# Sums over features in the norms of a three-layer fp32 block: additions on GpSimd, then two matmuls, in place of eight matmuls

## The reference

```python
def layer_norm(x, g, b):                       # end of layers 1 and 2
    mu = jnp.mean(xf, axis=-1, keepdims=True)
    var = jnp.mean(jnp.square(xf - mu), axis=-1, keepdims=True)
    return (xf - mu) * lax.rsqrt(var + LN_EPS) * g + b

x_new = layer_norm(DEEPNORM_ALPHA * x + gate * y, ln_g, ln_b)     # y: the layer's output projection

def rmsnorm(x, g):                             # layer 3: four of these
    return xf * lax.rsqrt(jnp.mean(xf * xf, axis=-1, keepdims=True) + RMS_EPS) * g
```

## Time and profile before

| | |
|---|---|
| median of 3 runs | 3994.05 us (3992.76 to 3996.78) |
| profiled execution: first to last instruction | 3989.9 us |
| what lies around the span (median less span) | 4.15 us |
| TensorE matmuls busy | 3558.6 us (89%) |
| DVE, ACT, POOL busy | 1573.4 us (39%), 1315.7 us (33%), 70.2 us (2%) |
| mean granted TensorE clock | 0.932 of 2.4 GHz |

### The profile page before, as it was taken

One profiled execution on the slowest core, in us unless ns is written; L12 is line 12 of the kernel. 1 busy time (PEld: TensorE's weight loads), 2 busy tenths in 40 slices (PEclk: granted clock), 3 DMA queues, 4 the chain that ended last, 5 costly groups with the idle time before them and its releaser, 6 DMA issues.

```text
span 3989.9 us, 45425 instructions
## 1 busy us (share of the span) xinstructions
PE 3558.6 (89%) x18676; PEld 2754.5 (69%) x18676; DVE 1573.4 (39%) x3007; ACT 1315.7 (33%) x2213; POOL 70.2 (2%) x113
## 2 busy tenths in 40 slices
PE   9988888988979889988968889789888899999997
PEld 8866667767847667666737677666656678777885
DVE  3333343344354334444334455533333433323322
ACT  3122233333262223433353323322322433323322
POOL 1000000000000000000000000000000000000000
PEclk9988899898989889999989999899977999999998
DMA  5111101103331000102320000000001222223222
GB/s 199 64 39 40 54 22 44 44 22 113 103 109 43 27 32 22 32 22 74 108 81 28 17 17 17 27 22 27 27 16 48 79 91 95 76 88 111 95 90 69
DMA packets 61709, 232.57 MB, mean 58 GB/s; under 512 B 7162, under 2 KB 7288, under 8 KB 60736
## 3 DMA queue, kind: packets, MB, share of 16 engines
q1 hardware_dynamic: 47520, 170.94, 13.2%
q0 software_dynamic: 13984, 58.73, 4.2%
HBM read 208.80 MB, written 20.84 MB: 58 GB/s over the span
## 4 chain that ended last, share of the span: by engine, by line
PE 48%; DVE 7%; ACT 5%; issue 2%; DMA 0%; ACTq 0%; DVEq 0%; POOL 0%
PE bank L275 33%; PE bank L2153 2%; PE bank L2132 2%; PE bank L1839 1%; ACT ws L239 1%; PE bank L1189 1%; PE bank L1848 1%; PE bank L2141 1%; PE bank L1222 1%; PE bank L439 1%; DVE ws L247 1%; PE bank L1847 1%; DVE ar L1897 1%; PE bank L503 1%; PE bank L1192 0%
## 5 line engine op out<-in xcount | busy, mean ns | idle before, releaser
L275 PE MATMUL bank<-HH,ws 128*128 128x512 f32 (+1 forms) x5088 | 1143.9, 381 | 35.1 <-DVE HH L1552 18.9
L275 PEld LDWEIGHTS bank<-HH,ws 128*128 128x128 f32 x5088 | 892.1, 196 | 212.6 <-issue 39.2
L247 DVE TENSOR_TENSOR ws<-raw,ws 128x1024 fp32r<-128x1024 f32 (+1 forms) x282 | 341.1, 1210 | 940.9 <-ACT ws L239 940.3
L275 PE MATMUL bank<-HF,ws 128*128 128x512 f32 x2112 | 497.6, 398 | 11.5 <-DVE ws L247 11.5
L275 PE MATMUL bank<-H,ws 128*128 128x512 f32 x1776 | 476.2, 423 | 23.9 <-DVE ws L247 15.0
L275 PEld LDWEIGHTS bank<-HF,ws 128*128 128x128 f32 x2112 | 401.0, 190 | 107.9 <-DVE ws L247 12.4
L275 PEld LDWEIGHTS bank<-H,ws 128*128 128x128 f32 x1776 | 349.8, 201 | 117.9 <-DVE ws L247 17.1
L239 ACT ACTIVATE ws<-raw 128x1024 fp32r<-128x1024 f32 (+1 forms) x282 | 293.3, 1041 | 133.7 <-PE bank L275 130.3
L275 PE MATMUL bank<-FF,ws 128*128 128x512 f32 x1056 | 255.3, 402 | 4.4 <-DVE ws L247 4.4
L275 PEld LDWEIGHTS bank<-FF,ws 128*128 128x128 f32 x1056 | 200.3, 190 | 57.0 <-issue 5.8
L775 ACT ACTIVATE Y<-bank 128x256 f32<-128x256 f32 (+1 forms) x152 | 82.6, 544 | 381.1 <-PE bank L275 381.1
(11 more groups left out here) (375 smaller groups left out, 3945.2 us busy)
## 6 DMA issues: line engine op xcount, KB each, us to landing
raw<-in_win SPq DMA_DIRECT2D x96, 512.0 KB, 3.6
raw<-in_wmod SPq DMA_DIRECT2D x48, 512.0 KB, 4.6
raw<-in_wout SPq DMA_DIRECT2D x48, 512.0 KB, 3.6
raw<-in_wgate SPq DMA_DIRECT2D x44, 512.0 KB, 3.6
raw<-in_wup SPq DMA_DIRECT2D x44, 512.0 KB, 3.6
raw<-in_wdown SPq DMA_DIRECT2D x32, 512.0 KB, 3.5
x<-Y POOLq DMA_DIRECT2D x4, 2048.0 KB, 8.3
raw<-in_wdown SPq DMA_DIRECT2D x16, 384.0 KB, 3.1
```

The source lines that it names most:

```text
L247: dve.tensor_tensor(ws[:, b % SPLIT, 1, 0:n], raw[:, blk["r"] % RAW, 0:n], ws[:, b % SPLIT, 0, 0:n].bitcast(F32), ALU.subtract).then_inc(s ...
L275: mm = pe.matmul(bank[o % 2][:, 0:n], ws[:, b % SPLIT, wp, k * P:(k + 1) * P], blk["rhs"](xp, blk["k0"] + k, t0, n), start=blk["first"] an ...
```

## The change

The eight matmuls of a sum become a running sum on GpSimd and two matmuls. For squares (`SquareSum`), GpSimd adds tiles 0 to 6 elementwise in six additions; TensorE multiplies this total and tile 7, in one bank. ACT's square m now waits for GpSimd's addition m - 2, not for a matmul. For the layer norm's mean, GpSimd adds each residual tile when DVE has made it (seven additions, for all chunks of part a at once), and TensorE has one matmul. In the lists, the pair of matmuls comes later: after block 4 + c in layers 1 and 2, once after block 0 of part b and once at the end in layer 3's output, after block 5 for `ri`, after pair 19 in the FFN. GpSimd's list has the additions among its transfers; stores of the early chunks no longer wait for each other, and the last chunk's store stands behind the additions of the tail.

```diff
+        class SquareSum:
+            ADDS = KT - 2
...
+            def act_room(self, a, c, m):
+                if m == 0 and c:
+                    a.wait_ge(*self.s_add.at(self.ADDS * c))
+                elif m == 1 and c:
+                    a.wait_ge(*self.s_var.at(c))
+                elif m >= 2:
+                    a.wait_ge(*self.s_add.at(self.ADDS * c + max(1, m - 2)))
+
+            def pool_sum(self, g, c, tiles=range(1, KT - 1)):
+                for m in tiles:
+                    if m == 1 and c:
+                        g.wait_ge(*self.s_var.at(c))
+                    if m > 1:
+                        g.wait_ge(*self.s_add.at(self.ADDS * c + m - 1))
+                    g.wait_ge(*self.s_sq.at(c * KT + m + 1))
+                    one = self.sq[0] if m == 1 else self.total
+                    g.tensor_tensor(self.total, one, self.sq[m % 2], ALU.add).then_inc(self.s_add.sem, 1)
+
+            def pe_var(self, p, c):
+                n = self.chunks[c][1]
+                p.wait_ge(*self.s_add.at(self.ADDS * (c + 1)))
+                p.matmul(bank[self.bank0 + c][:, 0:n], self.mean(), self.total, start=True, stop=False)
+                p.wait_ge(*self.s_sq.at(KT * (c + 1)))
+                p.matmul(bank[self.bank0 + c][:, 0:n], self.mean(), self.sq[(KT - 1) % 2], start=False, stop=True).then_inc(self.s_var.sem, 1)
...
             def pe_mean(pt, c):
                 a_, b_ = seg(c)
-                pt.wait_ge(*s_res.at(KT * (NA if c < NA else NCK)))
-                for m in range(KT):
-                    mm = pt.matmul(bank[2 + 2 * c][:, 0:b_ - a_], k1("mean"), Y[:, m, a_:b_], start=m == 0, stop=m == KT - 1)
-                mm.then_inc(s_mu.sem, 1)
+                pt.wait_ge(*s_sum.at((KT - 1) * (1 if c < NA else 2)))
+                pt.matmul(bank[2 + 2 * c][:, 0:b_ - a_], k1("mean"), rsum[0][:, a_ - lo:b_ - lo] if c < NA else rsum[1], start=True, stop=True).then_inc(s_mu.sem, 1)
+
+            def pool_res(g, part, m):
+                a_, b_ = (lo, chunks[NA][0]) if part == 0 else seg(LAST)
+                g.wait_ge(*s_res.at(NA * (m + 1) if part == 0 else NA * KT + m + 1))
+                if m > 1:
+                    g.wait_ge(*s_sum.at((KT - 1) * part + m - 1))
+                if m:
+                    one = Y[:, 0, a_:b_] if m == 1 else rsum[part]
+                    g.tensor_tensor(rsum[part], one, Y[:, m, a_:b_], ALU.add).then_inc(s_sum.sem, 1)
...
                 g.dma_start(dst.ap()[:, :, a_:b_], Y[:, :, a_:b_]).then_inc(s_xst.sem, 16)
-                g.wait_ge(*s_xst.at(xst0 + 16 * (c + 1)))
...
                     if i >= 2:
-                        pt_, pm = divmod(i - 2, KT)
-                        g.wait_ge(*s_res.at(NA * (pm + 1) if pt_ == 0 else NA * KT + pm + 1))
+                        pool_res(g, *divmod(i - 2, KT))
                     a_, b_ = (lo, chunks[NA][0]) if part == 0 else seg(LAST)
                     g.dma_start(XS[i % 2][:, a_:b_], src[:, m, a_:b_]).then_inc(s_xs[i % 2].sem, 16)
+                    for c in range(NA):
+                        if part and m == 4 + c:
+                            stats[c].pool_sum(g, 0)
+                pool_res(g, 1, KT - 2)
+                pool_res(g, 1, KT - 1)
                 for c in range(NA):
                     store_chunk(g, c)
...
-                        if m == 3 + c:
-                            pe_var(pt, c)
-                if rms is not None:
-                    rms.pe_var(pt, 0)
+                        if m == 4 + c:
+                            stats[c].pe_var(pt, 0)
...
             def tail_pool(g):
+                if rms is not None:
+                    rms.stat.pool_sum(g, 0)
+                stats[LAST].pool_sum(g, 0)
+                if rms is not None:
+                    rms.stat.pool_sum(g, 1)
+                g.wait_ge(*s_xst.at(xst0 + 16 * NA))
                 store_chunk(g, LAST)
+                g.wait_ge(*s_xst.at(xst0 + 16 * NCK))
...
                 fill()
                 fill()
-                pe_var(pt, LAST)
+                if rms is not None:
+                    rms.stat.pe_var(pt, 0)
+                stats[LAST].pe_var(pt, 0)
...
                     if c:
+                        ro.stat.pool_sum(g, 0)
+                        ro.stat.pool_sum(g, 1, range(1, 3))
                         g.wait_ge(*ro.x_done(0, KT - 1))
...
+                ro.stat.pool_sum(g, 1, range(3, 5))
+                ri.stat.pool_sum(g, 0)
+                ro.stat.pool_sum(g, 1, range(5, KT - 1))
...
-                    if m:
-                        ro.pe_var(p, 0, m - 1)
                 for m, blk in enumerate(part_b):
                     whole(pe_block(p, blk))
-                    ro.pe_var(p, *((1, m - 1) if m else (0, KT - 1)))
-                    if m == 4:
-                        ri.pe_var(p, 0)
-                ro.pe_var(p, 1, KT - 1)
+                    if m == 0:
+                        ro.stat.pe_var(p, 0)
+                    if m == 5:
+                        ri.stat.pe_var(p, 0)
+                ro.stat.pe_var(p, 1)
...
-                    if nxt and j == NORM:
-                        nxt.pe_var(p, 0)
+                    if nxt and j == NORM + 1:
+                        nxt.stat.pe_var(p, 0)
...
-                    if m:
-                        rout.pe_var(p, 0, m - 1)
-                rout.pe_var(p, 0, KT - 1)
+                rout.stat.pe_var(p, 0)
```

More of the change, by code:

```diff
@@ L143, in at, with of @@
         return self.sem, self.base + n
+    def of(self, n):
+        return Count(self.sem, self.base + n)
 class Chain:
@@ L418, in __init__ @@
                 nk = len(chunks) * KT
-                self.s_sq, self.s_var, self.s_rt, self.s_hi, self.s_lo = (sem(x, nk) for x in "r_sq r_var r_rt r_hi r_lo".split())
+                self.s_sq, self.s_rt, self.s_hi, self.s_lo = (sem(x, nk) for x in "r_sq r_rt r_hi r_lo".split())
                 self.s_rs, self.s_ln = sem("r_rs", len(chunks)), sem("r_ln", len(chunks))
+                self.stat = SquareSum(chunks, sq, total, self.s_sq, mean, bank0, "r")
                 self.done = self.s_lo.at(nk)
@@ L476, in build, with __init__ @@
         class NormOut:
-            def __init__(self, gi, chunks, src, add, sq, rs, mean, eps, bank0):
+            def __init__(self, gi, chunks, src, add, sq, rs, mean, eps, bank0, total):
                 self.gi, self.chunks, self.src, self.add, self.sq, self.rs = gi, chunks, src, add, sq, rs
@@ L482, in __init__ @@
                 nk = len(chunks) * KT
-                self.s_sq, self.s_var, self.s_t, self.s_x = (sem(x, nk) for x in "p_sq p_var p_t p_x".split())
+                self.s_sq, self.s_t, self.s_x = (sem(x, nk) for x in "p_sq p_t p_x".split())
                 self.s_rs, self.s_ln = sem("p_rs", len(chunks)), sem("p_ln", len(chunks))
+                self.stat = SquareSum(chunks, sq, total, self.s_sq, mean, bank0, "p")
             def x_done(self, c, m):
@@ L493, in act_square @@
                 a.wait_ge(*need)
-                if i >= 2:
-                    a.wait_ge(*self.s_var.at(i - 1))
+                self.stat.act_room(a, c, m)
                 sq = self.sq[i % 2]
                 a.activation(sq, like(self.src(m, t0, n), sq), ACT.Square).then_inc(self.s_sq.sem, 1)
[L499 to L503, removed]
             def act_rstd(self, a, c):
                 n = self.chunks[c][1]
-                a.wait_ge(*self.s_var.at((c + 1) * KT))
+                a.wait_ge(*self.stat.s_var.at(c + 1))
                 if c:
@@ L2443, in store @@
             def store(g):
+                if nxt:
+                    nxt.stat.pool_sum(g, 0)
+                rout.stat.pool_sum(g, 0)
                 g.wait_ge(*rout.x_done(0, KT - 1))
```

55 lines of the change are left out of this document (30 added, 25 removed).

## The result

The changed kernel takes 3964.3 us (median; 3963.1 to 3966.0), the kernel before 3994.95 in the same comparison. The ratio is 0.9922, with a 95% interval of 0.9907 to 0.9936: 30.7 us faster, where 36 were forecast (3958, from 35.7 on the span). The time lies in the range 3935 to 3986. The profiled spans differ by 27.5 us (3989.9 and 3962.4).

A forecast was written before the change was run, and what follows sets the result against it. TensorE, busy 89% of the span, was taken as the bound. Gains of 8.0 - 2.3 + 8.9 + 9.1 + 12.0 = 35.7 us took the span 3989.9 to 3954.2, plus 4.15 gives 3958; range 3935 to 3986.

The forecast's parts named there:

- Removed work and its price: TensorE, all norms: 113 matmuls go, 0.86 us each at 512 columns, 0.43 at 256, together 92 us at most.
- The addition's price: GpSimd: 1.2 us for an addition of 512 elements, a pace of 1.3 with the semaphore, bounds 0.8 and 1.5.
- A sum's length: Sums of squares on GpSimd: the last addition is done 7.8 us after the second square.
- Layer 1: Output projection and norm: ACT free 9.9 us earlier in part b, collisions 1.4, tail 0.5 later; gain 8.0 us.
- Layer 2: Output: part b gains 10.5 us, the tail with three sums in series loses 12.8; together -2.3 us.
- Layer 3: Output projection: 7.7 us from nine fewer matmuls between blocks, 1.2 at the FFN's input norm; sum 8.9 us.
- sum done 11.6 after that block's end: Layer 3's output: the sum on ACT's RMS squares is done 11.6 us after block m=4 ends.
- FFN: Second half's input norm gains 9.1 us; output norms gain 6.0 in each half, 12.0.
- From span to time: Whole kernel: the median of the runs is 4.15 us above the span, so 3954.2 gives 3958.
- the first rival: GpSimd and DVE hinder each other: 3974 us if a third of 47 additions wait, 3991 if most; chance 0.15.
- The reversal by price: Rival, slower than before: 35.7 us are gone at 2.06 us per addition with hand-over; 4010 at 2.4; chance 0.10.
- All of TensorE's time coming back: Rival, whole kernel: 92 us return, 3902, or about 3925 with half of the new waits; chance 0.07.

The follow-up runs named there:

- `first_gap`: The changed kernel, but ACT writes the square of tile 0 directly into the running sum: 3966.6 us against 3993.5 before, ratio 0.9937.
- `hybrid`: The changed kernel, but five sums of squares with no weight blocks beside them are TensorE's eight matmuls again: 3942.5 us against 3989.55 before, ratio 0.9878.
- `doubled`: The changed kernel with each of the 78 additions of squares preceded by another of the same size: 4030.25 us against 3989.55 before, ratio 1.0105.
- `all_three`: The changed kernel with square 0 written into the sum, layer 3's GpSimd sums queued earlier and layer 2's constants issued earlier: 3964.95 us against 3993.5 before.

## Why the forecast was right, and where not

- **Removed work and its price.** 113 matmuls went, and the busy time fell by 99 us (92 were reckoned from starts). Right.
- **The addition's price.** 1.2 and a pace of 1.3 were taken; 1277 ns and 1.33 to 1.34 came. The Trainium skill's proportion (GPSIMD Engine Reference, section 3.1), an estimate of 1.12, was too low; the measurement decides.
- **A sum's length.** Mis-sized: 7.8 us from the second square to the last addition. It is 8.7 to 8.8, since behind the first addition GpSimd waits 0.87 for ACT's third square (shown by `first_gap`).
- **Layer 1, 8.0 against 2.7.** Part b came by the mechanism reckoned, but smaller: ACT's eviction moved by 8.0 (9.9 forecast). Then 3.5 were given back: 0.95 each by two collisions of the last residual additions with DVE's L1518 (1.4 for both was in the forecast), and 1.6 by a first block that took longer behind TensorE's wait. The tail was costed at 0.5 loss and lost 1.8. `hybrid` recovers 2.8.
- **Layer 2, -2.3 against -3.5.** Part b 10.5 and 10.7. The tail -12.8 and -14.2; from block 7's end to the second block of the next unit 85 us came where 83.5 were forecast. `hybrid` shows that the three sums are the cause.
- **Layer 3, 8.9 against 0.9.** The 7.7 us between the blocks came (7.8 at the end of m=4). The failed step is "sum done 11.6 after that block's end": TensorE could go on with it 16.9 after the eviction at 3122.09. 4.4 of the difference are the late start, as the additions were held by DVE's row of residual instructions, and 0.9 the idle piece behind the first addition. I had weighed this exclusion as a rival and held against it that DVE mostly waits during the sums; here it does not.
- **FFN, 21.1 against 19.0.** The input norm right (9.1, 8.5); the output norms 5.3 each in place of 6.0.
- **Not in the sum:** 3.9 us from the clock of layer 2's attention, and by medians some 5 us more that go with the new outputs of layers 1 and 2 and stay open.
- **From span to time.** The 4.15 us that were added are 1.8 to 2.1 in every run of which both are known; some 2 us of the forecast's 3958 were scatter of the one profiled execution.
- **The range.** It was said to leave 0.12 above it. By its own chances it leaves at least 0.18: 0.11 for slower and 0.07 for the first rival's 3991.

So the total is right in part by luck. The changed stages gave 19 of the 36 us forecast, and gains that no term of the sum had brought the medians to 28 to 31.

The rivals: the hindrance between GpSimd and DVE is real, but it did not fall evenly on a third of the 47 additions. It cost layer 3 some 4 to 5 us and layer 1 another 2. The reversal by price exists, as `doubled` shows. A straight line from a pace of 1.34 (28 us faster) to 2.46 (41 us slower) crosses zero at about 1.8, an estimate, where the forecast had 2.06. All of TensorE's time coming back was far off.

## What to carry to other kernels

Moving a reduction from a busy engine to a slower idle one pays where other work of the busy engine stands beside it, and loses where that engine only waits for the result: here 13 sums moved gave 28 to 31 us, 8 of them gave 47 (each with the five means). Reckon each place by itself, and leave those with nothing beside them. And read a wait in the idle column with care: what stands behind it may be held by something else all the same.

## What the runs showed of the hardware

An addition on GpSimd and a DVE instruction with two SBUF inputs lengthen each other where they meet. DVE's remainder of 1.23 us had a mean of 1.83 beside a row of additions, and DVE's row without a gap kept an addition of 1.26 for up to 5.34 us. That additions in a row keep DVE out for more than the one it meets was not seen. An fp32 addition of 512 elements took 1.26 us for two tiles and 1.04 for a tile with itself. TensorE's granted clock fell to 0.79 behind an idle piece of 2.52 us (7.41 in place of 5.84 for a block), and filling one such piece moved the low clock to the next; yet behind 3.55 us in `hybrid` a block ran in 5.84, so the length of the piece alone does not tell. A change of stage can shift the granted clock 350 us later (0.97 to 1.00), in three of three profiles of one comparison, but not in `all_three`. Unchanged code of layer 3's mixing part differed by up to 8.5 us from profile to profile, so gains of 1 to 3 us can be read only by stage.
